# Linear attention: moving the next pair's mixing and key square to later places of the doubling levels

## What is computed

```python
zs = z + (jnp.pad(z, ((0, 0), (1, 0), (0, 0)))[:, :S] - z) * mu      # mixing
r, k, v, wd, ad, gd = _split(zs, ...)
kk = heads(k * k_k)
kk = kk / jnp.maximum(jnp.sqrt(jnp.sum(kk * kk, axis=-1, keepdims=True)), 1e-12)
...
y = rwkv7_scan(rh, heads(decay), kh, vh, -kk, kk * ah)
mean = jnp.mean(y, axis=-1, keepdims=True)
var = jnp.mean(jnp.square(y - mean), axis=-1, keepdims=True)
y = ((y - mean) * lax.rsqrt(var + GN_EPS)).reshape(B, S, RW_DIM) * gn_w + gn_b
```

## Time and profile before

| | |
|---|---|
| median of 3 runs | 3938.89 us |
| lowest and highest | 3933.21 and 3941.79 us |
| profiled execution, first to last instruction (span) | 3931.4 us |
| granted TensorE clock, mean over the span | 0.979 |
| PE busy | 3743.9 us (95%) |
| DVE, ACT, POOL busy | 1848.1, 1581.7, 1779.5 us |

### The profile page before, as it was taken

The page is one execution under the profiler, slowest core; times in us unless marked ns, Lnnn a source line. Parts: engine busy times, 40 slices in busy tenths (PEclk is TensorE's granted clock), DMA queues, the critical chain, the costliest instruction groups (busy, mean ns, idle before and its releaser), DMA issues. The chain is left out here.

```text
span 3931.4 us, 72626 instructions
## 1 busy us (share of the span) xinstructions
PE 3743.9 (95%) x30890; PEld 3040.7 (77%) x30904; DVE 1848.1 (47%) x2868; ACT 1581.7 (40%) x2643; POOL 1779.5 (45%) x1132
## 2 busy tenths in 40 slices
PE   7999989999998999998999999899999999999998
PEld 6777758878887777776887887677878877787887
DVE  7777652155635877754226553543231133423112
ACT  5555352343334555535234333454332234433222
POOL 5555444434445555544443444463444435344443
PEclk9999999989998999999998999899999999999999
DMA  4111203335532211122334553212222221222322
GB/s 142 52 56 56 88 28 135 99 134 193 183 107 76 92 51 56 56 99 72 99 105 143 189 182 104 69 65 76 97 86 97 97 85 66 70 96 87 97 97 86
DMA packets 108753, 379.88 MB, mean 97 GB/s; under 512 B 12560, under 2 KB 12944, under 8 KB 107792
## 3 DMA queue, kind: packets, MB, share of 16 engines
q1 hardware_dynamic: 102816, 365.66, 27.8%
q10 hardware_dynamic: 5616, 9.58, 0.7%
HBM read 359.46 MB, written 15.73 MB: 95 GB/s over the span
## 5 line engine op out<-in xcount | busy, mean ns | idle before, releaser
L299 POOL TENSOR_TENSOR Wlo<-raw,Whi 128x1024 fp32r<-128x1024 f32 (+1 forms) x744 | 1385.8, 1876 | 1671.6 <-ACT Whi L284 1671.4
L232 PE MATMUL ps<-hh,Whi 128*128 128x512 f32 x2864 | 1150.9, 402 | 22.1 <-DVE hl L383 10.1
L232 PE MATMUL ps<-hl,Whi 128*128 128x512 f32 x2864 | 1125.3, 393 | 0.0
L232 PE MATMUL ps<-hh,Wlo 128*128 128x512 f32 x2864 | 1124.4, 393 | 0.1
L284 ACT ACTIVATE Whi<-raw 128x1024 fp32r<-128x1024 f32 x552 | 578.7, 1054 | 689.3 <-PE ps L232 617.8
L232 PEld LDWEIGHTS ps<-hh,Whi 128*128 128x128 f32 x2864 | 543.3, 190 | 147.8 <-issue 15.7
L232 PEld LDWEIGHTS ps<-hh,Wlo 128*128 128x128 f32 x2864 | 543.0, 190 | 116.2 <-issue 0.5
L232 PEld LDWEIGHTS ps<-hl,Whi 128*128 128x128 f32 x2864 | 543.8, 190 | 108.1 <-issue 1.9
L232 PE MATMUL ps<-gh,Whi 128*128 128x512 f32 x864 | 337.9, 391 | 3.8 <-POOL Wlo L299 3.8
L232 PE MATMUL ps<-gh,Wlo 128*128 128x512 f32 x864 | 336.5, 390 | 0.0
L232 PE MATMUL ps<-gl,Whi 128*128 128x512 f32 x864 | 336.5, 389 | 0.0
(11 more groups left out here) (365 smaller groups left out, 5652.8 us busy)
## 6 DMA issues: line engine op xcount, KB each, us to landing
raw<-in_stream SPq DMA_DIRECT2D x554, 512.0 KB, 3.3
ada<-in_ada SPq DMA_DIRECT2D x96, 512.0 KB, 4.3
park_x<-xT SPq DMA_DIRECT2D x2, 2048.0 KB, 7.3
park_yh<-yh ACTq DMA_DIRECT2D x16, 256.0 KB, 2.1
park_yl<-yl ACTq DMA_DIRECT2D x16, 256.0 KB, 2.5
xT<-park_x SPq DMA_DIRECT2D x2, 2048.0 KB, 8.3
yrh<-park_yh SPq DMA_DIRECT2D x16, 256.0 KB, 5.1
yrl<-park_yl SPq DMA_DIRECT2D x16, 256.0 KB, 4.9
```

The costliest lines, as they stand in the source:

```text
L232: last = pe.matmul(ps, left[a](k), right[c](k), start=start and k == 0 and i == 0, stop=stop and k == n - 1 and i == 2)
L299: last = pool.tensor_tensor(b["Wlo"][:, slot, part], b["raw"][:, raw_slot(b, u), part], b["Whi"][:, slot, part].bitcast(F32), SUB)
```

## The change

For the next pair, the mixing of k and `kkr` go on DVE from behind the scans (level 0) to behind the deviation and `cm` (level 1); the mixing of r goes from behind level 1 to behind level 2, ahead of the mixing of v. On ACT the square `sqk` goes from ahead of `en` and `f` (behind level 1) to behind the copy of GV (behind level 2). The two step tables follow this order for all pairs but the first. Nothing is added or removed.

```diff
-PREP_V = Steps("c0", "c1", "c2", "c3", "kkr", "cx", "big", "rn", "kk", "b", "na", "nr", "kf", "ks", "rk",
+PREP_V = Steps("c0", "c1", "c2", "c3", "cx", "kkr", "big", "rn", "kk", "b", "na", "nr", "kf", "ks", "rk",
...
-PREP_A = Steps("sqk", "en", "f", "ep", "epx", "rt", first=("sqk", "rt", "en", "f", "ep", "epx"))
+PREP_A = Steps("en", "f", "sqk", "ep", "epx", "rt", first=("sqk", "rt", "en", "f", "ep", "epx"))
...
         def between(l):
             if l == 1 and p + 1 < PAIRS:
-                rwkv_prep_act(act, s, b, p + 1)
                 rwkv_exps_act(act, s, b, p + 1, ("en", "f"))
             if l == 2:
                 rwkv_gv_act(act, s, b, p)
+                if p + 1 < PAIRS:
+                    rwkv_prep_act(act, s, b, p + 1)
                 if p:
                     rwkv_post_act(act, s, b, p - 1)
...
         def between(l):
             if p + 1 < PAIRS and l == 0:
                 rwkv_scan_dve(dve, s, b, p + 1)
-                rwkv_mix_dve(dve, s, b, p + 1, "k")
-                rwkv_kk_dve(dve, s, b, p + 1)
             if l == 1 and p:
                 rwkv_mean_dve(dve, s, b, p - 1)
             if p + 1 < PAIRS:
                 if l == 1:
                     rwkv_prep1_dve(dve, s, b, p + 1)
+                    rwkv_mix_dve(dve, s, b, p + 1, "k")
+                    rwkv_kk_dve(dve, s, b, p + 1)
+                if l == 2:
                     rwkv_mix_dve(dve, s, b, p + 1, "r")
-                if l == 2:
                     rwkv_mix_dve(dve, s, b, p + 1, "v")
```

## The result

| | before | change |
|---|---|---|
| median of 4 runs | 3938.39 us | 3896.62 us |
| lowest and highest | 3933.21 and 3941.79 | 3896.09 and 3898.36 |
| span of the profiled execution | 3931.4 | 3896.6 |

The ratio is 0.9894, with a 95% interval of 0.988 to 0.9908: faster by 41.8 us, where 32.4 were forecast.

The account below looks back on a forecast made before the run. PE was taken to bound the kernel, so only its waits could be won: 12 x 2.34 + 2 x 2.15 = 32.4 us off 3931.4 gives 3899.0, plus 7.5 is 3906.5 us; range 3900 to 3918.

Parts of the forecast that it names:

- The wait for the deviation: At level 2 of pairs 1 to 6, PE's wait goes, 2.34 us, twelve times; the deviation comes 0.82 us early.
- the sum: Closed level-2 waits: 28.1 us for pairs 1 to 6 plus 4.3 for pair 0, 32.4 us in all.
- Pair 0: At level 2 of pair 0, PE's waits for X (0.75 us) and Wc (1.40) go: 2.15 us, twice.
- What is late next: Moved work still fits: ACT for level-3 Wc by 0.4 us, DVE additions for level 4 by 0.8, r copy free.
- A rule against it: Shared-port rule: each of four DVE instructions could pay a whole POOL piece, at least 0.716 us; trace shows 0.48 more.
- the first rival: 20%: DVE's four instructions each pay a whole POOL piece; at level 3 twelve pairs lose 0.8 us, 9.6 back, 3916.
- The failed step: The runs' median stays 7.5 us above the profiled span, so the forecast span of 3899.0 us becomes 3906.5.

Follow-up runs that it names:

- e2: The kernel before, with nine added 128x512 matmuls on PE ahead of level 2 in pairs 1 to 6; 3929.55 us, ratio 0.998.
- e3: The change, with PE waiting at the head of level 2 in pairs 1 to 6 for the next pair's mixing of k; 3931.49 us.
- e4: The change on DVE alone, with ACT's order as in the kernel before; 3996.36 us, ratio 1.0146.
- e6: The change, but with the mixing of r left behind level 1, now behind kkr; 3904.13 us.

## Why the prediction was right and wrong

**The wait for the deviation: right.** 0.82 us of cover were forecast and 0.82 measured. e2 puts the closed waits, pair 0's with them, at 32.9 us, where the sum said 32.4. **Pair 0: right**; neither wait is in the trace of the change.

**What is late next: right that it fits, a little too cautious.** `cm` took 0.68 us, not the 1.15 assumed, though POOL's pieces (138.37 to 142.11) lay beside it; `dz` right behind it took 1.22. ACT had 0.78 us left where 0.4 were forecast. At level 3 the first addition ended at 148.32, 1.9 us ahead of PE at 150.23; 0.8 were forecast. By the Trainium skill's rule on the shared SBUF ports ("SBUF — State Buffer", section "SBUF: two separate sides") each of the four could pay a whole POOL piece, and "A rule against it" found the measured 0.48 us too small for it. The trace of the change agrees better than that. Two POOL pieces; their median is 0.736 us:

```profile
139.77 1.20 POOL L299 TENSOR_TENSOR Wlo<-raw,Whi 128x256 fp32r<-128x256 f32 x1
```

```profile
140.94 1.17 POOL L299 TENSOR_TENSOR Wlo<-raw,Whi 128x256 fp32r<-128x256 f32 x1
```

`cm` started at 139.71, just ahead of the first, and paid nothing; that POOL piece was the loser and took 1.20 us. `dz` and k started while a piece ran, and each ended 0.55 us after that piece (141.53 after 140.97, 142.66 after 142.11). So the DVE instruction pays what is left of the piece that it meets, 0.3 to 0.5 us here, and not a whole one: the worst case that the first rival was built on needs every instruction to start just behind the start of a piece.

**The failed step: "The median of the runs shown is 7.5 us above the span; with that kept, 3906.5 us."** The 7.5 us were not a fixed offset. About 1.8 us are; the other 5.7 were time that the profiled execution happened to have less of, and the change removes such time. And the sum of 32.4 left out the three falls that even this execution had: the prediction put the clock at nothing, since the mean over 380 us was 1.00. The 9.9 us between 3906.5 and 3896.6 are these two: 5.7, and 4.2 for three falls. The term that was missing is the clock behind the waits. Measured, it is 8.3 us (e2 against before, same job), and 32.9 + 8.3 = 41.2 of the 41.8. At some 1.5 us a fall that is five or six falls in a typical execution; the four profiles show three to six, and three of the four took less than the medians of 3937 to 3938.

That the falls come from the waits is shown from both sides: filling the waits takes the falls and 8 us away (e2), putting them back brings falls back (e3, two in its profile), and at twice their length a fall comes at every one (e4). Not only the profiled executions say so: the mean granted clock over the whole span, averaged over the executions of a job, is 0.9776 to 0.9781 in the kernel before (26, 15, 11 and 7 executions), 0.9794 with the waits filled (11), 0.9775 with the wait put back (11) and 0.980 in the change (4 and 4). The Trainium skill ("TensorE: Matmul & The Clock Gate", section "Part 1: The HAM clock gate") says that a gate lowers TensorE's clock by how busy it has been of late, and that the moment varies from run to run. The traces agree, with 0.50 behind some waits and not behind others of the same length.

**Open:** why 3 to 6 of 12 nearly equal waits are followed by a fall, what the part of e3's 10 us is that its three falls do not cover, what e6's other 3.7 us are, and what makes the spread of the change outside its pairs.

## What to carry to other kernels

A wait of the busiest engine costs its length and, on TensorE, it can cost the clock behind it. Look for it in windows of a few us behind each wait: a mean over a stage prints 1.00 while it costs 8 us in all. Before a sum is tied to one profiled execution, ask where that one stands among the runs and what the others have more of. If it is the fastest, a change that removes waits will gain more than its trace shows. And when instructions go to later places, look at every engine that waits for them: here ACT's `sqk` had to move too, and DVE's part alone cost 58 us (e4).

## What was not expected of the hardware

- A stop of 2.1 to 2.3 us of TensorE between dense matmuls is enough for the granted clock to go to 0.50, and it does so behind 3 to 6 of the 12 stops of a profile (three of the 48 lasted 3.0 us). None came behind the waits of 0.7 to 1.2 us of pairs 0 and 7 in the four profiles of before.
- At a stop of 4.7 to 5.6 us it fell in each of 14 (e4), at some 2.1 us each beside the stop.
- Nine wasted 128x512 matmuls in each of 12 waits made the program 8.3 us faster (e2).
- Beside POOL, a DVE instruction lost only the rest of the POOL piece that it met; where it came first, the POOL piece was the longer one, 1.20 us instead of 0.74.
